# Delta chunks of two output blocks set around the Hyena norm, the mLSTM norm in parts, and the queries' decay on GpSimd

## The reference

```python
def odd_mixer(h, ...):                     # first transformer, layer 1
    hm = mlstm_chunkwise(q_m, k_m, v_m, i_pre, f_pre)        # 4 heads of 128
    hm = jax.nn.sigmoid(o_m) * hm
    hm = rmsnorm(hm, ml_norm_g)                              # head by head
    ha = mla_attention(...)                                  # 8 heads of 64
    return jnp.concatenate([hm, ha], axis=-1) @ w_out

for i in range(DEPTH):                     # second transformer
    x = x + 0.5 * _swiglu(_rmsnorm(x, ffn1_norm[i]), ...)
    proj = _rmsnorm(x, mix_norm[i]) @ w_in[i]
    o_dn = _deltanet_group(q, k, v, z, beta_logit, alpha, ...)     # 512 wide
    o_hy = _hyena_group(hy_in, ...)                                # 512 wide, ends in _rmsnorm(zz, norm_w)
    x = x + jnp.concatenate([o_dn, o_hy], axis=-1) @ w_out[i]
    x = x + 0.5 * _swiglu(_rmsnorm(x, ffn2_norm[i]), ...)
```

## Time and profile before

| | |
|---|---|
| median of three runs | 4165.9 us (4156.64, 4165.9, 4167.36) |
| profiled execution, its own time | 4161.18 us |
| its span in the trace | 4159.4 us |
| TensorE busy | 3829.6 us (92%) |
| TensorE weight loads | 3073.3 us (74%) |
| VectorE busy | 2068.1 us (50%) |
| ScalarE busy | 1096.8 us (26%) |
| GpSimd busy | 48.0 us (1%) |
| mean granted clock of TensorE | 0.952 |

### The profile page before, as it was taken

How to read it: one execution, slowest core, us unless ns; L and a number is a source line. 1 busy time by engine, 2 the same in 40 slices (tenths; PEclk the granted TensorE clock), 3 DMA queues, 4 the chain that set the end, 5 groups by cost and what they waited for, 6 DMA issues and landing times.

```text
span 4159.4 us, 42350 instructions
## 1 busy us (share of the span) xinstructions
PE 3829.6 (92%) x17182; PEld 3073.3 (74%) x17182; DVE 2068.1 (50%) x2589; ACT 1096.8 (26%) x1218; POOL 48.0 (1%) x65
## 2 busy tenths in 40 slices
PE   8889999978979998999998979999999998979998
PEld 6677888745758887888775757887888775857886
DVE  4555444363455434453656565444443656565433
ACT  2232222133332222222242312222222243312221
POOL 0000000000000000000000000000000000000000
PEclk9899999978999998999999989999999999989999
DMA  3122222210212221222312112222222312112221
GB/s 123 65 71 81 101 96 89 72 41 1 85 54 101 101 91 61 101 88 96 118 61 91 61 56 86 101 96 87 100 93 89 130 61 92 62 51 87 95 96 66
DMA packets 66781, 342.88 MB, mean 82 GB/s; under 512 B 23524, under 2 KB 23524, under 8 KB 30816
## 3 DMA queue, kind: packets, MB, share of 16 engines
q1 hardware_dynamic: 60864, 303.19, 20.9%
q0 software_dynamic: 5792, 37.92, 2.4%
HBM read 324.31 MB, written 16.78 MB: 82 GB/s over the span
## 4 chain that ended last, share of the span: by engine, by line
PE 83%; DVE 11%; ACT 2%; issue 2%; DMA 1%; SPq 0%; DVEq 0%; ACTq 0%
PE ACC L943 24%; PE ACC L945 24%; PE ACC L944 24%; PE MIX L1017 1%; PE ACC L1461 1%; PE ACC L1201 1%; DVE WL L2040 1%; PE MIX L1034 1%; DVE BX L2544 1%; DVE BT L2542 1%; PE ACC L1181 1%; PE MIX L1113 1%; DVE PT L2734 0%; DVE PT L2732 0%; DMA RAW<-wall 0%
## 5 line engine op out<-in xcount | busy, mean ns | idle before, releaser
L943 PE MATMUL ACC<-HH,WH 128*128 128x512 f32 (+1 forms) x3322 | 1317.9, 397 | 92.3 <-issue 27.8
L944 PE MATMUL ACC<-HL,WH 128*128 128x512 f32 (+1 forms) x3322 | 1302.5, 392 | 0.0
L945 PE MATMUL ACC<-HH,WL 128*128 128x512 f32 (+1 forms) x3322 | 1301.1, 392 | 0.0
L2040 DVE TENSOR_TENSOR WL<-RAW,WH 128x2048 fp32r<-128x2048 f32 x292 | 668.2, 2288 | 507.7 <-ACT WH L1620 506.8
L943 PEld LDWEIGHTS ACC<-HH,WH 128*128 128x128 f32 x3322 | 635.3, 191 | 254.0 <-issue 76.6
L944 PEld LDWEIGHTS ACC<-HL,WH 128*128 128x128 f32 x3322 | 636.1, 191 | 131.2 <-issue 3.1
L945 PEld LDWEIGHTS ACC<-HH,WL 128*128 128x128 f32 x3322 | 634.6, 191 | 132.0
L1620 ACT ACTIVATE WH<-RAW 128x2048 fp32r<-128x2048 f32 x292 | 556.2, 1906 | 596.6 <-PE ACC L945 592.2
L945 PE MATMUL ACC<-HIDH,WL 128*128 128x512 f32 x1056 | 421.3, 399 | 0.0
L944 PE MATMUL ACC<-HIDL,WH 128*128 128x512 f32 x1056 | 416.1, 394 | 0.0
L943 PE MATMUL ACC<-HIDH,WH 128*128 128x512 f32 x1056 | 414.0, 392 | 0.0
(11 more groups left out here) (474 smaller groups left out, 3011.7 us busy)
## 6 DMA issues: line engine op xcount, KB each, us to landing
RAW<-wall SPq DMA_DIRECT2D x261, 1024.0 KB, 4.8
RAW<-wall SPq DMA_DIRECT2D x24, 768.0 KB, 4.1
KR<-spectra POOLq DMA_DIRECT2D x4, 2048.0 KB, 9.4
x_kept<-X POOLq DMA_DIRECT2D x2, 2048.0 KB, 6.7
FWK<-mats POOLq DMA_DIRECT2D x4, 1024.0 KB, 5.3
spectra<-SQ POOLq DMA_DIRECT2D x8, 512.0 KB, 2.9
spectra<-T POOLq DMA_DIRECT2D x8, 512.0 KB, 3.5
X<-x_kept POOLq DMA_DIRECT2D x2, 2048.0 KB, 14.6
```

What stands on the lines that cost most here:

```text
L943: pe.matmul(out_ap, wh, hh, start=first, stop=False)
L944: pe.matmul(out_ap, wh, hl, start=False, stop=False)
L945: return pe.matmul(out_ap, wl, hh, start=False, stop=last)
L2040: v.tensor_tensor(WL[n % 2][:], RAW[n % 2][:], WH[n % 2][:], ALU.subtract).then_inc(w_lo, 1)
```

## The change

There are three independent parts.

**Output layer (twice).** `pe_norm` no longer does anything for the Hyena norm; its TensorE steps are in `joined_opening`, between products of the first two output blocks with the delta chunks. The unit of the second block is split ahead: `split_hi` at the end of ScalarE's Hyena function, `split_lo` at the end of VectorE's, ahead of the norm's adds. In layer 0, where the first output block has ACC banks 2 and 3, the last inverse runs its banks in the order 2, 3, 0, 1, so that the block's banks come free first; VectorE follows.

**Opening of the delta stage (twice).** `grown_queries` leaves VectorE. It is now GpSimd's, in the same order of heads, with a count of two in `dn_qe` per head. ScalarE's `decays(h)` for h of 2 and 3 waits for both operations of head h-2, and TensorE waits for all eight before the first values behind the solve. The diff, cut to its core:

```diff
@@ schedule @@
+        def head_sums(h):
+            return MIX[:, 2, :] if h < 3 else ACC[:, 3 if after_cells % 2 == 0 else 0, :]
+        def bank_order(st, n):
+            turned = n % 2 and hyena_out[st.layer].b0 % 2
+            return (2, 3, 0, 1) if turned else (0, 1, 2, 3)
@@ GpSimd @@
+                    for h in range(4):
+                        pool.wait_ge(dn_e1, 4 * l + h + 1)
+                        pool.tensor_tensor(E1[:, h, :], E1[:, h, :], DQ[:, h, :], ALU.mult).then_inc(dn_qe, 1)
+                        pool.wait_ge(dn_kq, 4 * l + h + 1)
+                        pool.wait_ge(dn_qe, 8 * l + 2 * h + 1)
+                        pool.tensor_tensor(DQ[:, h, :], DQ[:, h, :], T[:, h % 2, :], ALU.mult).then_inc(dn_qe, 1)
@@ TensorE @@
+            def joined_opening(st, norm):
+                pe.wait_ge(h_ready, norm.h0)
+                pe.wait_ge(hy_z, 8 * norm.nrm_hy + 6)
+                pe.wait_ge(w_lo, st.u0 + 1)
+                products(0, range(2), range(4))
+                sum_paired(norm)
+                pe.wait_ge(hy_z, 8 * norm.nrm_hy + 8)
+                pe.wait_ge(w_lo, st.u0 + 2)
+                products(1, [0], range(4))
+                late_scale(norm)
+                products(1, [1], range(4))
+                for c in range(4):
+                    pe.wait_ge(h_ready, norm.h0 + c + 1)
+                    last = products(0, range(2), [4 + c])
+                last.then_inc(unit_done, 1)
+                products(1, range(2), range(4, 8)).then_inc(unit_done, 1)
+            def mixed_block(st, bank, wh, wl):
+                cell = st.hall - 4
+                for k in range(4, 8):
+                    products(k, cell)
+                head_squares(3)
+                for k in range(2):
+                    products(k, cell + k + 1)
+                head_scale(2)
+                head_scale(3)
+                products(2, cell + 3)
+                return products(3, cell + 4)
             def pe_norm(st):
+                if st.src == "HY":
+                    return
@@ pe_delta @@
+                pe.wait_ge(dn_qe, 8 * L + 8)
                 values(0, 0)
@@ pe_mlstm @@
+                for h in range(3):
+                    head(h + 1)
+                    sums(h)
+                    if h:
+                        head_squares(h - 1)
+                head_squares(2)
+                sums(3)
+                head_scale(0)
+                head_scale(1)
@@ ScalarE: decays, end of act_hyena, act_linear, end of act_mlstm @@
-                        act.wait_ge(dn_qe, o - 1)
+                        act.wait_ge(dn_qe, 2 * (o - 1))
                 split_hi(st.next_unit, 0, 0)
+                split_hi(st.next_unit + 1, 0, 0)
+                                if st.joins and i == 0:
+                                    if j == 0:
+                                        split_hi(n + 2, add, i)
+                                    continue
+                root(0, (0, 1, 2))
                 square_head(3)
+                hi_chunks(st.h0, [0])
+                root(1, (3,))
+                hi_chunks(st.h0, range(4), first=1)
@@ VectorE: dve_mlstm, dve_delta, dve_hyena @@
+                for h in range(3):
+                    weights(h)
+                    gated(h)
+                weights(3)
+                statistics(0, (0, 1, 2))
+                v.wait_ge(ml_sw, 4)
+                diagonal(0)
+                diagonal(1)
+                gated(3)
+                out_head(st, 0)
+                statistics(1, (3,))
+                diagonal(2)
+                out_head(st, 1)
+                diagonal(3)
+                out_head(st, 2)
                 out_head(st, 3)
                     matrices(h)
-                    grown_queries(h)
+                    for at, m in enumerate(bank_order(st, n)):
+                        v.wait_ge(hy_y, 4 * n + at + 1)
+                split_lo(st.next_unit + 1, 0, 0)
```

## The result

The changed kernel took 4123.49 us (median of 4 runs, 4118.28 to 4126.54) against 4166.63 us before (median of 4, 4156.64 to 4168.32): a ratio of 0.9904, 95% interval 0.9891 to 0.9916. Forecast were 4119 and a range of 4104 to 4136. The traced execution of after has a span of 4121.8, 37.6 less than the 4159.4 before, where the sum had said 44.0. A right total, then, but it will turn out that its terms are not all right.

What follows compares the result with a forecast made beforehand. TensorE, with 83% of the chain that ended last, was taken as the bound, so only its idle or half-clock time counts. From 4161.2, −35.0 − 5.5 − 3.5 = −44.0 gave 4117.2, plus 1.6 made 4119 us; range 4104 to 4136.

Steps and rivals of the forecast that it cites:

- Output layer: Both output layers: delta-chunk products fill TensorE's idle time after the inverse; −17.5 us per layer, −35.0 for both.
- the sum: All three parts together: −35.0 − 5.5 − 3.5 = −44.0 us from the profiled execution's 4161.2.
- the third block's split: Output layer: the third block's weights, split after their buffer comes free, are ready with 1.3 us in hand.
- mLSTM's end: Once, behind the mLSTM: 24 attention products run before the last heads finish; −6.9 us, taken as −5.5 for half clock.
- one of the signs given: At the mLSTM: block 1 of the layer behind it starts before 1057 us, against 1061.94 in the kernel before.
- Opening: Delta opening, twice: eight VectorE query multiplications per layer go to GpSimd; −1.74 us per layer, −3.5 in all.
- GpSimd's price: Delta opening, per 128×512 multiplication: 1.4 us by elements per partition, 2.8 by all elements; 2.8 was taken.
- Rival 1: Delta opening: VectorE and GpSimd hold each other up, 2.8 us per layer; −3.5 becomes +2.1, total 4124.4; chance 0.12.
- Rival 2: End of the mLSTM: head 3's squares wait behind 24 matmuls at half clock; −5.5 becomes 0, total 4124.3; chance 0.08.
- Rival 3: Output layers yield half, through half clock or late third-block weights; −17.5 for both, total 4136 us; chance 0.06.
- Rival 4: Delta opening: GpSimd multiplications far dearer, head 3 slipping beyond 3.6 us each; 4181.5 at 11 us each; chance 0.02.

Runs made afterwards that it cites:

- again: The changed kernel, unaltered, run a second time for another trace; 4116.89 us against 4165.89 before, ratio 0.9885.
- c_off: The changed kernel with the delta opening's query multiplications on VectorE again instead of GpSimd; median 4124.4 us.
- best_again: Second run of the changed kernel with head 3's squares ahead of the 24 attention products and the second block's weights split early at the mLSTM's end; median 4120.9 us.
- pool_busy: The changed kernel with each GpSimd query multiplication preceded by three multiplications of the same tile by 1.0; median 4132.6 us.
- one_block: The changed kernel with only the first output block's delta products ahead, none of block 1 between sums, scale and chunks; median 4138.2 us.

## Why the prediction was right, point by point

- **Output layer: right, nearly to the row.** Forecast for layer 0 were the end of block 0 at 18.8 and of block 1 at 24.3 us behind the inverse's end; measured 18.7 and 24.1. The waits forecast as 0.4 and none were 0.17 and none, the third block's split ended 1.15 before block 1 (forecast 1.3). −17.7 and −18.2 for −17.5 each. In layer 1 the kernel before lost 0.5 more in its first block, at a granted clock of 0.80 there for 0.83.
- **mLSTM's end: right in kind, too large.** Forecast −6.9 from the order of the steps and −5.5 with 1.4 for half clock; by the landmark it is −4.0 (−3.0 with the early stretch). Block 1 began at 1058.35 in "again" and not before 1057, one of the signs given. What was mis-sized is the half clock. With T as the end of the last numerator (there LU of head 3 starts), T is at 38.9 instead of 37.6. The squares of head 2, moved ahead of the last sums, wait 0.66 for ScalarE and take 1.05, but before TensorE had stood idle at that place:

```profile
1023.88 2.49 PE L1570 MATMUL MIX<-ONES,LW 128*128 128x1 f32 x20 [1.39 <-DVE LW L2423]
```

The sums start 1.54 us behind the start of head 3's weights before and 1.71 in "again", so the moved step costs 0.2. The other 1.0 is clock: sums and numerator take 2.90 and 4.61 us for 2.49 and 4.00. In c_off, the same code here, T is at 37.8. The last head was ready at T + 22.6 for T + 21.4; there the six products of chunk 1 took 2.4 us for 1.4 and the scales behind them 2.61 for the 1.88 that best_again shows. The squares ended at T + 8.6, as forecast; block 1 began at T + 26.2 for T + 24.8. By subtraction (−6.9 + 0.2 against −4.0), half clock took 2.7 us where 1.4 was allowed.
- **Opening: right, the size a little too small.** Forecast −1.74 per layer; measured 2.0 to 2.1 at equal clock and 3.7 where a second half-clock stretch goes too, which the sum had only as a bound. GpSimd's price was taken from the wrong end of its bounds: 1.27 to 1.40 is the value by elements per partition, and the 2.77 that both ends came from had some 0.36 of waiting for VectorE in it.
- **Rival 1** didn't happen, although its mechanism exists (pool_busy), and stood already in the earlier trace rows, which the prediction took as evidence against it: the eight short operations hardly meet the instructions with two SBUF inputs. **Rival 2**, nothing from the mixed block, was what the first two traces seemed to show (−0.1), and was wrong: a half-clock stretch in one of them. **Rival 3** didn't happen, the clock stayed up, but one_block shows how near it was: without block 1's products between the steps it falls. **Rival 4**: the slack was real, 3.6 for head 3 and 3.1 for head 2.
- **The sum.** By landmarks, the opening at the clock of the kernel before (3.7 and 1.9): −35.9 − 4.0 − 5.6 = −45.5 against the forecast's −44.0. The total is as near as it is because errors of opposite sign cancel in part: the mLSTM's 1.5 too much against 0.9 too little for the output layers and 2.1 for the opening. The first trace's −37.6 is this with the half clock that fell on the one execution and not the other: 3.9 us in the mLSTM, 4.2 behind the solve of layer 0, 0.9 behind that of layer 1; the last 1.1 I didn't follow. Of medians, −43.1 and −49.0.

What sets a half-clock stretch off at 0.83 us of idle time in one execution and not in the other stays open, and with it whether the queries on GpSimd have a part in it.

## What to carry to other kernels

Work that fills the idle time between short dependent steps can be worth more than its length where it also keeps TensorE at its upper clock: here 5.4 us of products brought 8.2 to 8.5. When a step is moved ahead of another, look for the idle time that was there before (head 2's squares cost 0.2 us and not their 1.7), and ask of every step behind a filling whether a chain on another engine hangs on it (head 3's squares: 5.9 us for a change of order). And when a row is taken as the price of an instruction, see what ran beside it: the 2.77 of the earlier trace rows was 2.41 and a wait. Never read an edit's worth from one pair of traces: take a landmark ahead of the edit that tells the clock, read the granted clock behind it too, and compare executions that agree on both.

## What the runs showed of the hardware

- The same kernel runs a stretch at half clock in some executions and not in others: head 3's scores took 2.32 or 4.00 us, in six of the twelve traces the weights of head 3 were late by it; an idle time of 0.83 us preceded full clock in six traces and half clock in six, in layer 0. Such stretches cost 3 to 4 us each here.
- In the delta opening, TensorE's idle time before the third turn of the queries was followed by half clock in all five readings where it was 2.84 to 3.11 us, and in none of the others, where it was 1.4 to 2.2.
- GpSimd multiplies 128×512 by 128×512 in 1.27 us, and by two constants of 1.0, in place, in 0.67. VectorE takes 0.68 for the first. The 0.67 isn't a rule for constants: 64×1024 times −1.0 took 2.78 in every trace.
- GpSimd and VectorE hold each other up where VectorE has two SBUF inputs: +0.84 on 2.02 for GpSimd, +0.16 to +0.97 for VectorE; and 64×1024 on GpSimd took 2.41, 2.77 and 3.08 us with overlaps of 0.08, 0.49 and 0.81.
